# Moving the spatial bias from TensorE to VectorE in a two-layer decoder step, with a new order of gate evictions, row loads, softmax and projection

## The chip, the cores and the metric

The kernel runs on one core of one Trainium2 chip. The metric is the device time of one launch in microseconds (us), the median of several runs; lower is better. The engines: TensorE (PE, matmuls and transposes), VectorE (DVE), ScalarE (ACT), GpSimd (POOL, here mostly gathers and scatters by indirect DMA), SyncE (SP, issues most loads). Each engine runs its own queue of instructions in order, and the kernel ties them together with semaphores by hand.

## The reference, cut

One step of a two-layer decoder for 512 prompt tokens and 8 x 8 sample tokens, 576 rows of 1024. Layer 0 has the chunked gMLP mixer, layer 1 a short convolution; each layer then has 16 experts (two per token) and a per-layer-embedding gate.

```python
# layer 0's mixer; chunks of 128 rows, 4 heads, width 3072
z = gelu(x @ w_in + b_in);  u, v = split(z)
v = layer_norm(v, ln_g, ln_b)
sg = einsum("hts,bcshd->bcthd", tril(w_s), v) + transpose(b_s)[:, :, None]
mix = (u * sg) @ w_out
# every layer
x = layer_norm(alpha * x + mixer(x), ln1_g, ln1_b)
g_logits = x @ w_group + b_group;  e_logits = x @ w_expert + b_expert
# best of 4 groups, two best of its 4 experts; weight = softmax of the two * softmax of the group
moe = sum over the two experts e of weight_e * (silu(x @ w_gate_e) * (x @ w_up_e)) @ w_down_e
x = layer_norm(alpha * x + moe, ln2_g, ln2_b)
x = x + sigmoid(x @ ple_w_gate + ple_b_gate) * (p @ ple_w_proj)
```

## The kernel before, in words

**Numbers.** Every fp32 operand of a matmul is split into a high and a low part of a shorter type (x_hi, x_lo, w_hi, w_lo): ScalarE makes the high part (hi, L848), VectorE the low part (lo, L1166), and PE makes three products per term (L1741 to L1743, L2062 to L2064). Weights come in units of 1 MB (w_raw), which SP loads as their buffers come free, and each unit is split by one hi and one lo of 2048 columns.

**Stages.** V part of the mixer (to 176 us), then six rounds of four tiles of the A width (to 499), then the last output rows with first LayerNorm and router (to 575), 16 experts (to 737), addition of the experts' rows, second LayerNorm and gate (to 820); layer 1 has its convolution and then the same stages from the router on, with the same code, and each is some 501.6 us behind its place in layer 0.

**The mixer's rounds.** For each tile fl of a round PE makes u (u_tile) and the spatial product (spatial, L1854 to L1859) into PSUM banks b and b+1. The head's bias is put there first, by two matmuls of ones_r (all ones, one contraction row that holds the bias) with b_spatial. VectorE's gate_product multiplies u by it in place (L1257, L1258), ScalarE makes the high part (L902), g_low the low part (L1265). PE's out_tiles begins with the first three tiles' products for two output tiles (36 matmuls) before it waits for the fourth tile's low part.

**Router.** h_turns(i) transposes row tile i, logits(i) multiplies by the router's weights; the tiles 0 to 4 follow each other, 4 being the 64 rows left over. Then PE has the projection p @ w_proj in eight tiles (proj), among which stand ranks(1) (L1960, L1963: each token's rank in its expert, from the one-hot that VectorE writes at L1372) and the matmuls L2019 that turn ranks to slots. VectorE makes slot indices from them (L1430), GpSimd gathers the first expert's rows.

**Experts.** moe_step(s): ScalarE splits two weight units, then Silu on gate (L1003), VectorE multiplies by up (L1499), PE transposes the product (L2091), and then has gate_up of the next expert (L2062). Ahead of the first expert VectorE computes the softmax weights (L1457 to L1483), ScalarE two exponentials (L974, L976).

**Second LayerNorm and gate.** y_out copies an expert's result (L987, L989), GpSimd scatters it to y_scratch in DRAM. SP loads the four gate units (gate_load) and the rows of y (rows_load, one per row tile, both experts of each token). VectorE adds the rows (add_rows, L1572) and the last two experts' rows through PE (add_last, L1580; their low parts are L1560 and L1629), ScalarE the squares (L1046) and the standard deviation (L1051). The norm is on ScalarE (L1056) for tiles 0, 2, 3, 4 and on VectorE (L1590) for tile 1. PE turns the rows (n2_turn_rows, L2183), both scale them into xT, and 16 gate tiles follow: q 0 to 7 are the eight output tiles for the first 256 rows, 8 to 15 for the other 320. Tiles q and q+4 share a PSUM bank of the first eight, in its two halves. ScalarE evicts each by a sigmoid (L1081), VectorE finishes it (L1618, L1619).

Of the kernel before, what the change touches and what calls it, by code (L numbers as in the profile page):

```python
# [5 lines left out]
P = 128  # L6
D = 1024
KT = D // P
TP, TS = 512, 64
T = TP + TS  # L10
NT = 5
HALF = T // 2
AW = 3072
NH = 4
# [63 lines left out]
def trunk(nc, x_in, outs):  # L78
# [63 lines left out]
    bsx = new("b_spatial", [P, NH, P + TS], f32r)  # L142
# [21 lines left out]
    bsrc = at("b_spatial_src", [1, NH, P], f32, S0 + 23040)  # L164
    bss = at("b_spatial_all", [1, NH, P + TS], f32, S0 + 25088)
    bsl = at("b_spatial_low", [1, NH, P + TS], f32r, S0 + 28160)
# [5 lines left out]
    gf = at("g_full", [P, 2, T], f32, S0 + 18432)  # L172
    vc = at("v_cols", [P, NT, 512], f32, S0 + 23040)
# [138 lines left out]
    with ctx:  # L312
# [9 lines left out]
        blk_ld, bsl_ld = sem("blocks_loaded"), sem("bias_low_loaded")  # L322
# [12 lines left out]
        bs_ok, bsh_ok, bsl_ok, ones_ok = sem("bias_spread"), sem("bias_high"), sem("bias_low"), sem("ones_ready")  # L335
# [154 lines left out]
        HALVED = (0, 1, 3, 4)  # L490
# [15 lines left out]
        def _(sp):  # L506
# [40 lines left out]
            for l in range(DEPTH):  # L547
# [42 lines left out]
                for j in range(3):  # L590
                    gate_load(j)
# [65 lines left out]
        def _(pool):  # L657
# [20 lines left out]
            pool.dma_start(bsrc[:, :, :], x_in["a_b_s"]).then_inc(ws_ld, 16)  # L678
# [46 lines left out]
            pool.wait_ge(bsl_ok, 1)  # L725
            pool.dma_start(bsx[1:2, :, :], bsl[:, :, :]).then_inc(bsl_ld, 16)
            pool.wait_ge(bsl_ld, 16)
# [27 lines left out]
            for l in range(DEPTH):  # L755
# [47 lines left out]
                for s in range(4, NE):  # L803
                    gather(s)
                    expert_rows(s - 4)
                    if s in (6, 9):
                        n = (s - 6) // 3
                        pool.wait_ge(w_ok, 2 * (l + 1))
# [33 lines left out]
        def _(act):  # L842
# [37 lines left out]
            act.wait_ge(bs_ok, 1)  # L880
            act.activation(bsx[0:1, :, :], bss[:, :, :], ACT.Copy).then_inc(bsh_ok, 1)
# [45 lines left out]
            for l in range(DEPTH):  # L927
# [11 lines left out]
                def proj_out(mo):  # L939
                    act.wait_ge(mt_done, M_P[l] + mo + 1)  # L940
# [22 lines left out]
                rows_hi(4)  # L963
                proj_out(0)
                proj_out(1)
# [5 lines left out]
                xT_hi(0, bank=4)  # L971
                proj_out(KT - 1)
# [3 lines left out]
                act.activation(gm[:, 1, :], gm[:, 1, :], ACT.Exp).then_inc(r_ex_ok, 1)  # L976

# [83 lines left out]
                def scale(i):  # L1061
                    t, b = tok(i), turned_bank(TR_N2[l] + i)
                    act.wait_ge(n2_turn, NT * l + i + 1)
                    for k in range(0 if i == 2 else 4, KT):
# [5 lines left out]
                def tile_hi(i):  # L1070
                    if i != 2:
                        act.wait_ge(n2_scaled, 4 * l + HALVED.index(i) + 1)
# [1239 lines left out]
```

## Time and profile before

| | |
|---|---|
| median of 3 runs | 1335.91 us (1332.87 to 1340.4) |
| profiled execution: its own time, span | 1331.28 us, 1329.7 us |
| mean granted TensorE clock | 0.971 |
| busy: PE, VectorE, ScalarE, GpSimd | 94%, 61%, 44%, 16% |
| moved by DMA | 229.52 MB |

Busy time is the share of the span in which an engine executes something. The clock is a share of 2.4 GHz; a stretch in which it is near 0.5 runs at 1.2 GHz.

### The profile page before, as it was taken

How to read it: one execution, taken by the hardware profiler on the slowest of the kernel's cores; microseconds unless marked ns; L12 is line 12 of the kernel's file. 1: busy time of each engine (PE TensorE's matmuls, PEld its weight loads, DVE VectorE, ACT ScalarE, POOL GpSimd, SP SyncE). 2: the span in 40 equal slices, each digit the busy share in tenths (PEclk: the TensorE clock that was granted, in tenths of full speed). 3: DMA queues.
4: the chain of work that ended last, by engine and by line, in shares of the span. 5: the costliest groups of instructions: out<-in, count | busy, mean ns of one | idle time of the engine just before them, and what ended most of it. 6: DMA issues, size and time to landing. Idle time of an engine off the chain costs nothing.

```text
span 1329.7 us, 19763 instructions
## 1 busy us (share of the span) xinstructions
PE 1254.0 (94%) x7729; PEld 1144.1 (86%) x7729; DVE 815.8 (61%) x1093; ACT 584.6 (44%) x650; POOL 213.6 (16%) x211
## 2 busy tenths in 40 slices
PE   6999999999999999989999599999999989999598
PEld 5888899999999998878878589999998878877488
DVE  4653476254453624779889766455434778888763
ACT  4322241212121223378888663212213368888661
POOL 2300011000000005322331001000004432232000
PEclk8999999999999999899999799999999899999799
DMA  9354344233242312379999453222312279998412
GB/s 315 130 180 140 130 145 143 80 127 114 75 146 75 122 68 66 104 286 349 374 386 337 159 163 100 70 91 80 110 67 66 87 276 348 385 393 323 172 49 71
DMA packets 85664, 229.52 MB, mean 173 GB/s; under 512 B 9878, under 2 KB 42814, under 8 KB 73184
## 3 DMA queue, kind: packets, MB, share of 16 engines
q1 hardware_dynamic: 66880, 179.84, 37.7%
q0 software_dynamic: 18720, 48.80, 10.6%
q8 instruction: 44, 0.72, 0.2%
q14 instruction: 20, 0.16, 0.0%
HBM read 209.90 MB, written 35.46 MB: 185 GB/s over the span
## 4 chain that ended last, share of the span: by engine, by line
PE 70%; DVE 11%; DMA 10%; ACT 6%; issue 2%; SPq 0%; DVEq 0%; ACTq 0%; POOLq 0%
PE ps L1741 13%; PE ps L1743 13%; PE ps L1742 13%; DMA w_raw<-in_moe_w_gate_up 5%; DVE w_lo L1166 3%; PE ps L1793 3%; PE ps L1794 3%; PE ps L1795 3%; DMA w_raw<-in_moe_w_down 2%; ACT w_hi L848 2%; PE ps L2062 2%; PE ps L2063 2%; PE ps L2064 2%; PE ps L1857 2%; DVE x_tok L1572 1%
## 5 line engine op out<-in xcount | busy, mean ns | idle before, releaser
L1166 DVE TENSOR_TENSOR w_lo<-w_raw,w_hi 128x2048 fp32r<-128x2048 f32 (+1 forms) x133 | 290.7, 2191 | 80.6 <-ACT w_hi L848 79.8
L1741 PE MATMUL ps<-x_hi,w_hi 128*128 128x288 f32 (+2 forms) x1024 | 308.6, 301 | 14.7 <-DVE x_lo L1606 8.6
L1743 PE MATMUL ps<-x_hi,w_lo 128*128 128x288 f32 (+2 forms) x1024 | 305.8, 299 | 0.0
L1742 PE MATMUL ps<-x_lo,w_hi 128*128 128x288 f32 (+2 forms) x1024 | 305.7, 299 | 0.0
L848 ACT ACTIVATE w_hi<-w_raw 128x2048 fp32r<-128x2048 f32 (+1 forms) x133 | 242.8, 1834 | 104.5 <-PE ps L1743 73.9
L1741 PEld LDWEIGHTS ps<-x_hi,w_hi 128*128 128x128 f32 x1024 | 196.7, 192 | 17.4 <-issue 15.8
L1742 PEld LDWEIGHTS ps<-x_lo,w_hi 128*128 128x128 f32 x1024 | 196.8, 192 | 0.0
L1743 PEld LDWEIGHTS ps<-x_hi,w_lo 128*128 128x128 f32 x1024 | 196.6, 192 | 0.0
L1741 PE MATMUL ps<-g_hi,w_hi 128*128 128x288 f32 x384 | 114.3, 298 | 3.4 <-DVE g_full L1717 2.7
L1743 PE MATMUL ps<-g_hi,w_lo 128*128 128x288 f32 x384 | 113.2, 295 | 0.0
L1742 PE MATMUL ps<-g_lo,w_hi 128*128 128x288 f32 x384 | 113.1, 295 | 0.0
L2062 PE MATMUL ps<-w_hi,xgT_hi 128*128 128x512 f32 x256 | 104.4, 408 | 8.4 <-DVE xgT_lo L1451 8.1
L2064 PE MATMUL ps<-w_hi,xgT_lo 128*128 128x512 f32 x256 | 101.4, 396 | 0.0
L2063 PE MATMUL ps<-w_lo,xgT_hi 128*128 128x512 f32 x256 | 101.1, 395 | 0.0
L1257 DVE TENSOR_TENSOR g_full<-g_full,ps 128x512 f32<-128x512 f32 x24 | 16.4, 685 | 118.9 <-PE ps L1859 118.9
L1793 PE MATMUL ps<-w_hi,x_hi 128*128 128x512 f32 x192 | 76.1, 396 | 5.7 <-DVE w_lo L1177 5.7
L897 ACT ACTIVATE g_full<-ps,cols 128x576 f32<-128x576 f32 x24 | 17.7, 737 | 135.9 <-PE ps L1743 135.9
L1741 PEld LDWEIGHTS ps<-g_hi,w_hi 128*128 128x128 f32 x384 | 72.0, 188 | 5.6 <-DVE g_full L1717 2.9
L786 POOL DMA_INDIRECT x_gathered<-x_scratch,slot_token x32 | 51.5, 1609 | 152.1 <-PE ps L2033 121.5
L1166 DVE TENSOR_TENSOR w_lo<-w_raw_more,w_hi 128x2048 fp32r<-128x2048 f32 x30 | 68.0, 2289 | 12.2 <-ACT w_hi L848 12.2
L1794 PE MATMUL ps<-w_lo,x_hi 128*128 128x512 f32 x192 | 75.4, 393 | 0.0
L1795 PE MATMUL ps<-w_hi,x_lo 128*128 128x512 f32 x192 | 75.4, 393 | 0.0
(311 smaller groups left out, 2313.4 us busy)
## 6 DMA issues: line engine op xcount, KB each, us to landing
w_raw<-in_moe_w_gate_up SPq DMA_DIRECT2D x34, 1024.0 KB, 9.9
w_raw<-in_moe_w_down SPq DMA_DIRECT2D x32, 1024.0 KB, 13.9
w_raw_more<-in_moe_w_gate_up SPq DMA_DIRECT2D x30, 1024.0 KB, 14.6
w_raw<-in_a_w_in SPq DMA_DIRECT2D x23, 1024.0 KB, 5.3
w_raw<-in_a_w_out SPq DMA_DIRECT2D x12, 1024.0 KB, 5.1
w_raw<-in_b_w_in SPq DMA_DIRECT2D x12, 1024.0 KB, 5.2
w_raw<-in_ple_w_gate SPq DMA_DIRECT2D x8, 1024.0 KB, 10.2
v_scratch<-v_stage POOLq DMA_DIRECT2D x6, 1024.0 KB, 4.8
```

The costliest lines, as they stand in the source:

```text
L786: pool.indirect_dma_start(out=xg[:, s % 2, :], out_offset=None, in_=x_dram[l][:, :], in_offset=bass.IndirectOffsetOnAxis(ap=idx[:, s:s + 1 ...
L848: act.activation(unit_of(whi, d), raw_unit(d), ACT.Copy).then_inc(hi_done, 1)
L1166: dve.tensor_tensor(unit_of(wlo, d), raw_unit(d), unit_of(whi, d).bitcast(f32), ALU.subtract).then_inc(split_done, 1)
L1741: pe.matmul(out, sh, mh, start=first, stop=False)
L1742: pe.matmul(out, sh, ml, start=False, stop=False)
L1743: ins = pe.matmul(out, sl, mh, start=False, stop=final)
L1793: pe.matmul(v_bank(i), xh_, wh, start=first, stop=False)
L1794: pe.matmul(v_bank(i), xh_, wl, start=False, stop=False)
L1795: ins = pe.matmul(v_bank(i), xl_, wh, start=False, stop=final)
L2062: pe.matmul(ps[:, 0, :], xs[0], ws[0], start=(a == 0 and k == 0), stop=False)
L2063: pe.matmul(ps[:, 0, :], xs[0], ws[1], start=False, stop=False)
L2064: ins = pe.matmul(ps[:, 0, :], xs[1], ws[0], start=False, stop=(a == 1 and k == 3))
```

## The change

1. The bias b_s is loaded once by a broadcasting DMA to all 128 partitions. PE's two bias matmuls per tile go, and so does the preparation of the bias (its high and low part on VectorE and ScalarE, a DMA, two waits). gate_product adds the bias to the spatial product from PSUM to a new tile gate_sum and then multiplies u by it.
2. Gate tiles are evicted in the order 0, 4, 1, 5, 2, 6, 3, 7, 8 to 15 (EVICTED), and gate(8) to gate(11) wait for 2, 4, 6, 8 evictions instead of 5, 6, 7, 8. The turns of tile 4 come behind gate(6) instead of gate(5).
3. The norm of tiles 2 to 4 goes to VectorE, and so does half of the scaling of tile 2.
4. SP issues gate_load(2) behind rows_load(1), and VectorE adds the first rows ahead of the last experts' low parts.
5. Softmax: the last experts' places and the group's softmax stand ahead of the first rows' low part on VectorE, the exponentials ahead of their high part on ScalarE; ScalarE loads the Silu table by a one-column activation before it waits for the first gate_up.
6. Projection tile 1 is made in two halves, around h_turns(4).

```diff
 # SP
-                for j in range(3):
+                for j in range(2):
                     gate_load(j)
...
                 rows_load(1)
+                gate_load(2)
 # POOL
+            pool.dma_start(bs[:, :, :], x_in["a_b_s"].to_broadcast([P, NH, P])).then_inc(bs_ld, 16)
 # ACT
+                    if s == 0 and not step:
+                        act.activation(warm[:, :], eps[:, :], ACT.Silu)
                     q = it * step + (NE * l + s)
                     act.wait_ge(eu_used, it * (3 * step) + (EU * l + gu_unit(s) + 2))
...
+                proj_out(1)
                 proj_out(0)
-                proj_out(1)
...
-                xT_hi(0, bank=4)
-                proj_out(KT - 1)
                 act.wait_ge(r_ex, 2 * l + 1)
                 act.activation(ex[:, :, :], ex[:, :, :], ACT.Exp).then_inc(r_ex_ok, 1)
                 act.wait_ge(r_ex, 2 * l + 2)
                 act.activation(gm[:, 1, :], gm[:, 1, :], ACT.Exp).then_inc(r_ex_ok, 1)
+                xT_hi(0, bank=4)
+                proj_out(KT - 1)
...
                 squares(2)
                 std_of(2)
-                norm(2)
                 squares(3)
                 std_of(3)
                 scale(2)
-                norm(3)
                 tile_hi(2)
+                hi(U_G[l] + 3)
                 squares(4)
                 std_of(4)
-                norm(4)
-                hi(U_G[l] + 3)
 # DVE, gate_product
-                dve.wait_ge(u_done, q + 1)
+                b = 4 + 2 * (fl % 2)
                 dve.wait_ge(sg_done, q + 1)
-                b = 4 + 2 * (fl % 2)
-                dve.tensor_tensor(gf[:, fl % 2, 0:TP], gf[:, fl % 2, 0:TP], ps[:, b, :], ALU.mult)
-                dve.tensor_tensor(gf[:, fl % 2, TP:T], gf[:, fl % 2, TP:T], ps[:, b + 1, 0:TS], ALU.mult).then_inc(gm_done, 1)
+                dve.tensor_tensor(gsum[:, 0:TP].rearrange("p (c t) -> p c t", t=P), ps[:, b, :].rearrange("p (c t) -> p c t", t=P), bias, ALU.add)
+                ch.link(dve.tensor_tensor(gsum[:, TP:T].rearrange("p (b t) -> p b t", t=SB),
+                                          ps[:, b + 1, 0:TS].rearrange("p (b t) -> p b t", t=SB), bias_s, ALU.add))
+                dve.wait_ge(u_done, q + 1)
+                dve.tensor_tensor(gf[:, fl % 2, :], gf[:, fl % 2, :], gsum[:, :], ALU.mult).then_inc(gm_done, 1)
 # PE, spatial
-                pe.matmul(ps[:, b, :].rearrange("p (c t) -> p c t", t=P), ones_r[:, :], row, start=True, stop=False)
-                pe.matmul(out_s, ones_r[:, :], row_s, start=True, stop=False)
 # PE, router
                 logits(3)
+                pe.wait_ge(nz_ok, 2 * NT * l + NT - 1)
+                proj_half(l, 1, 0)
                 h_turns(4)
+                proj_half(l, 1, 1).then_inc(mt_done, 1)
                 logits(4)
                 pe.wait_ge(nz_ok, 2 * NT * l + NT)
                 proj(l, 0)
-                proj(l, 1)
                 ranks(1)
 # PE, gate
                     if q >= KT:
-                        pe.wait_ge(sg_ok, GQ * l + q - 3)
+                        pe.wait_ge(sg_ok, GQ * l + (2 * (q - KT) + 2 if q < KT + 4 else q - 3))
...
-                    if q in (1, 4, 5):
-                        n2_turn_rows((1, 4, 5).index(q) + 2)
+                    if q in (1, 4, 6):
+                        n2_turn_rows((1, 4, 6).index(q) + 2)
```

The first place is VectorE's queue in the mixer's first round, around the first two tiles' gate products (g_full is u and then the product, g_lo its low part). Before:

```order
L1257 TENSOR_TENSOR g_full<-g_full,ps 128x512
L1258 TENSOR_TENSOR g_full<-g_full,ps 128x64
L1166 TENSOR_TENSOR w_lo<-w_raw,w_hi 128x2048
L1265 TENSOR_TENSOR g_lo<-g_full,g_hi 128x576
L1257 TENSOR_TENSOR g_full<-g_full,ps 128x512
```

and after, where the lines of the file have other numbers:

```order
L1244 TENSOR_TENSOR gate_sum<-ps,b_spatial 128x512
L1245 TENSOR_TENSOR gate_sum<-ps,b_spatial 128x64
L1248 TENSOR_TENSOR g_full<-g_full,gate_sum 128x576
L1159 TENSOR_TENSOR w_lo<-w_raw,w_hi 128x2048
L1255 TENSOR_TENSOR g_lo<-g_full,g_hi 128x576
```

Two multiplies from PSUM have become two additions from PSUM and one multiply between tiles in SBUF; the weight split and the low part follow as they did.

The second place is SP's queue between the experts' last weights and the rows of y (w_raw<-in_ple_w_gate is a gate unit, the loads from y_scratch are the row tiles 0, 1, 2). Before, with the overflow branch, which isn't taken, left out:

```order
L587 DMA w_raw<-in_ple_w_gate 128x8x256 [waits w_split_done] x3
...
L615 DMA w_raw_more<-y_scratch 128x2x1024 [waits zeros_stored,w_split_done,y_stored1,y_stored0]
L615 DMA x_gathered<-y_scratch 128x2x1024 [waits xg_turned]
L615 DMA w_raw<-y_scratch 128x2x1024 [waits w_split_done,y_stored1,y_stored0]
L615 DMA w_raw<-y_scratch 128x2x1024
```

and after:

```order
L585 DMA w_raw<-in_ple_w_gate 128x8x256 [waits w_split_done] x2
...
L613 DMA w_raw_more<-y_scratch 128x2x1024 [waits zeros_stored,w_split_done,y_stored1,y_stored0]
L613 DMA x_gathered<-y_scratch 128x2x1024 [waits xg_turned]
L585 DMA w_raw<-in_ple_w_gate 128x8x256 [waits w_split_done]
L613 DMA w_raw<-y_scratch 128x2x1024 [waits w_split_done,y_stored1,y_stored0]
```

The third gate unit has moved behind two row loads and behind their wait for stores of y.

The third place is VectorE's queue behind the last expert (last_y_lo is the low part of the last two experts' rows, x_tok the row tile). Before:

```order
L1560 SCALAR_TENSOR_TENSOR last_y_lo_166<-expert_y,slot_weight,last_y_hi_164 128x1024
L1629 SCALAR_TENSOR_TENSOR last_y_lo_167<-ps,slot_weight,last_y_hi_165 128x512 x2
L1572 SCALAR_TENSOR_TENSOR x_tok<-w_raw_more,top_weights,x_tok 128x1024 x2
L1580 SCALAR_TENSOR_TENSOR x_tok,row_sums<-ps,x_tok 128x1024
L1565 TENSOR_SCALAR mean_var<-row_sums 128x1
L1572 SCALAR_TENSOR_TENSOR x_tok<-x_gathered,top_weights,x_tok 128x1024
L1592 RECIPROCAL rstd<-rstd 128x1
L1593 TENSOR_TENSOR neg_mean_rstd<-mean_var,rstd 128x1
L1572 SCALAR_TENSOR_TENSOR x_tok<-x_gathered,top_weights,x_tok 128x1024
```

and after:

```order
L1559 SCALAR_TENSOR_TENSOR x_tok<-w_raw_more,top_weights,x_tok 128x1024
L1616 SCALAR_TENSOR_TENSOR last_y_lo_164<-expert_y,slot_weight,last_y_hi_162 128x1024
L1559 SCALAR_TENSOR_TENSOR x_tok<-w_raw_more,top_weights,x_tok 128x1024
L1622 SCALAR_TENSOR_TENSOR last_y_lo_165<-ps,slot_weight,last_y_hi_163 128x512 x2
L1559 SCALAR_TENSOR_TENSOR x_tok<-x_gathered,top_weights,x_tok 128x1024
L1567 SCALAR_TENSOR_TENSOR x_tok,row_sums<-ps,x_tok 128x1024
L1552 TENSOR_SCALAR mean_var<-row_sums 128x1
L1559 SCALAR_TENSOR_TENSOR x_tok<-x_gathered,top_weights,x_tok 128x1024
L1579 RECIPROCAL rstd<-rstd 128x1
L1580 TENSOR_TENSOR neg_mean_rstd<-mean_var,rstd 128x1
```

Both additions of tile 0 and the first of tile 1 have moved up, among the low parts; the second of tile 1 stands ahead of tile 0's reciprocal.

## Rows read from the trace of the kernel before

**Rows 1.** The page, part 4: shares of the chain that ended last
```profile
PE 70%; DVE 11%; DMA 10%; ACT 6%; issue 2%; SPq 0%; DVEq 0%; ACTq 0%; POOLq 0%
```
**Rows 2.** Windows: us, busy of PE, PEld, DVE, ACT, POOL, clock, DMA share, GB/s
```profile
186.00:499.00 313.00, 312.37 (x2304) 304.45 (x2302) 149.43 (x186) 69.04 (x67) 19.45 (x34) 1.00 0.33 109
...
620.00:735.00 115.00, 110.18 (x527) 91.44 (x526) 99.27 (x87) 93.66 (x93) 32.18 (x23) 1.00 0.94 359
```
**Rows 3.** PE's waits, whole run: us in total, times, longest
```profile
PE ps L2183 <- ACT x_tok L1056: 11.8, 2, 5.9
```
**Rows 4.** Timeline of PE, two of the mixer's tiles: start, duration, line, operation
```profile
246.01 0.50 PE L1854 MATMUL ps<-b_spatial,ones_r 128*128 x1
...
246.41 1.10 PE L1857 MATMUL ps<-w_spatial,v_cols 128*128 x8
...
262.54 0.39 PE L1854 MATMUL ps<-b_spatial,ones_r 128*128 x1
...
262.82 1.10 PE L1857 MATMUL ps<-w_spatial,v_cols 128*128 x8
```
**Rows 5.** Timeline of VectorE, the same tile; in brackets the idle time before
```profile
264.45 0.69 DVE L1257 TENSOR_TENSOR g_full<-g_full,ps 128x512 f32<-128x512 f32 x1 [4.30 <-PE ps L1859]
...
266.02 0.76 DVE L1265 TENSOR_TENSOR g_lo<-g_full,g_hi 128x576 fp32r<-128x576 f32 x1 [0.75 <-ACT g_hi L902]
```
**Rows 6.** Timeline of PE, router
```profile
548.05 0.71 PE L1942 MATMUL ps<-ident,x_tok 64*128 64x64 f32 x8 [1.37 <-ACT x_tok L925]
550.17 0.32 PE L1952 MATMUL ps<-w_router_scaled,x1T_hi 128*128 128x120 f32 x1 [1.41 <-DVE x1T_lo L1339]
...
558.38 0.21 PE L1960 MATMUL ps<-expert_onehot,below_r 128*128 128x96 f32 x1
```
**Rows 7.** Windows: router, first experts, gates
```profile
550.00:557.00 7.00, 6.83 (x32) 6.83 (x33) 6.76 (x14) 0.59 (x1) 4.83 (x4) 0.55 0.35 112
...
584.00:588.00 4.00, 3.31 (x9) 2.62 (x9) 4.00 (x5) 2.43 (x3) 0.99 (x2) 0.60 1.02 425
...
789.00:793.00 4.00, 4.00 (x19) 4.00 (x19) 2.34 (x7) 0.95 (x2) 0.00 (x0) 0.58 0.93 292
```
**Rows 8.** Timeline of VectorE, router
```profile
557.11 0.21 DVE L1372 SCALAR_TENSOR_TENSOR expert_onehot<-places,group_onehot 128x48 fp32r<-128x48 f32 x1
```
**Rows 9.** Timeline of ScalarE, first expert
```profile
579.91 1.28 ACT L1003 ACT_TABLE_LOAD   x1
581.21 0.38 ACT L1003 ACTIVATE expert_act<-ps 128x256 f32<-128x256 f32 x1
```
**Rows 10.** Timeline of VectorE, first expert
```profile
583.07 0.41 DVE L1499 TENSOR_TENSOR expert_act<-expert_act,ps 128x256 f32<-128x256 f32 x1
```
**Rows 11.** Timeline of PE, first expert
```profile
584.73 0.72 PE L2062 MATMUL ps<-w_hi,xgT_hi 128*128 128x512 f32 x1 [0.69 <-DVE xgT_lo L1451]
```
**Rows 12.** DMA issues, 724 to 746 and 741 to 746 us: median us to landing
```profile
x_gathered<-y_scratch SPq DMA_DIRECT2D x1, 1024.0 KB, 8.8
...
y_scratch<-expert_y,slot_row POOLq DMA_INDIRECT x1, 7.3
...
y_scratch<-expert_y,slot_row_late POOLq DMA_INDIRECT x1, 3.2
```
**Rows 13.** Timeline of GpSimd, end of the experts
```profile
725.50 1.31 POOL L792 DMA_INDIRECT y_scratch<-expert_y,slot_row  x1 [8.33 <-ACT expert_y L989]
```
**Rows 14.** Timeline of ScalarE, head of the gate stage
```profile
738.33 1.92 ACT L848 ACTIVATE w_hi<-w_raw 128x2048 fp32r<-128x2048 f32 x1
...
743.31 1.15 ACT L1046 ACTIVATE w_raw_more<-x_tok,mean_var 128x1024 f32<-128x1024 f32 x1 [0.64 <-DVE mean_var L1565]
...
748.03 1.15 ACT L1046 ACTIVATE x_gathered<-x_tok,mean_var 128x1024 f32<-128x1024 f32 x1 [1.41 <-DVE mean_var L1565]
```
**Rows 15.** Timeline of VectorE, head of the gate stage
```profile
739.23 2.60 DVE L1572 SCALAR_TENSOR_TENSOR x_tok<-w_raw_more,top_weights,x_tok 128x1024 f32<-128x1024 f32 x2
```
**Rows 16.** Timeline of PE, the ninth gate tile
```profile
788.18 0.38 PE L1741 MATMUL ps<-x_hi,w_hi 128*128 128x320 f32 x1 [3.05 <-ACT ple_gate L1081]
```

More of the change, by code:

```diff
@@ L141, in trunk @@
     wss = new("w_spatial_s", [TS, NH, TS])
-    bsx = new("b_spatial", [P, NH, P + TS], f32r)
+    bs = new("b_spatial", [P, NH, P])
     vstat = new("v_stats", [P, NT, VP, 6])
@@ L172, in trunk @@
     gf = at("g_full", [P, 2, T], f32, S0 + 18432)
+    gsum = at("gate_sum", [P, T], f32, S0 + 37376)
     vc = at("v_cols", [P, NT, 512], f32, S0 + 23040)
@@ L489, in trunk @@
         LAST_BANK = (6, 2)
-        HALVED = (0, 1, 3, 4)
+        EVICTED = (0, 4, 1, 5, 2, 6, 3, 7) + tuple(range(KT, GQ))
         V_DONE = NT * VP
@@ L1063, in scale @@
                     act.wait_ge(n2_turn, NT * l + i + 1)
-                    for k in range(0 if i == 2 else 4, KT):
+                    for k in range(4, KT):
                         c = KT * l + k
@@ L1445, in _ @@
                 dve.tensor_scalar(ovf_e[:, :], ovf_f[0:1, :], float(NE - 1), None, ALU.min).then_inc(ovf_ok, 1)
-                def xT_lo(s, it=0, step=0, bank=2):
-                    q = it * (2 * step) + 2 * (NE * l + s)
-                    for b in range(2):
-                        dve.wait_ge(eth_ok, q + (b + 1))
-                        dve.tensor_tensor(eTl[:, 512 * b:512 * b + 512], ps[:, bank + b, :], eTh[:, 512 * b:512 * b + 512].bitcast(f32),
-                                          ALU.subtract).then_inc(etl_ok, 1)
-                xT_lo(0, bank=4)
+                late_v = row_v[:, NE - 2:NE]
+                ch.link(dve.scalar_tensor_tensor(out=last_at[:, 0, :], in0=shift[:, NE - 2:NE], scalar=float(T), in1=late_v, op0=ALU.add, op1=ALU.subtract))
+                dve.tensor_scalar(last_at[:, 1, :], last_at[:, 0, :], -float(P), None, ALU.add)
+                ch.link(dve.tensor_scalar(last_at[:, 2, :], last_at[:, 0, :], PA - 0.5, 2.0 * T, ALU.is_lt, ALU.mult))
+                ch.link(dve.tensor_tensor(last_at[:, 3, :], last_at[:, 2, :], late_v, ALU.add))
+                dve.tensor_scalar(row_zero[:, :], last_at[:, 3, :], -1.0, 4.0 * T, ALU.mult, ALU.add)
+                dve.scalar_tensor_tensor(out=row_late[:, :], in0=last_at[:, 2, :], scalar=2.0 * T, in1=late_v, op0=ALU.add, op1=ALU.subtract)
                 grp = lg[:, :, 0, :]
@@ L1466, in _, with xT_lo @@
                     dve.tensor_copy(ranks[:, a:b, :], ranks_of(a, b))
+                def xT_lo(s, it=0, step=0, bank=2):
+                    q = it * (2 * step) + 2 * (NE * l + s)
+                    for b in range(2):
+                        dve.wait_ge(eth_ok, q + (b + 1))
+                        dve.tensor_tensor(eTl[:, 512 * b:512 * b + 512], ps[:, bank + b, :], eTh[:, 512 * b:512 * b + 512].bitcast(f32),
+                                          ALU.subtract).then_inc(etl_ok, 1)
+                xT_lo(0, bank=4)
                 dve.wait_ge(r_ex_ok, 2 * (l + 1))
@@ L1650, in _ @@
                 rstd2(3)
+                scale2(2)
                 add_rows(4, 0)
@@ L2035, in turn_slots, with proj_half @@
                         ins.then_inc(xtp, 1)
+            def proj_half(l, mo, h):
+                if h == 0:
+                    pe.wait_ge(split_done, U_P[l] + mo // 2 + 1)
+                return products(ps[:, 2 * (mo % 2) + h, 0:HALF], [(w8(whi, mo // 2, k, P * (mo % 2)), w8(wlo, mo // 2, k, P * (mo % 2)),
+                                                                 gview(pThi, k, h), gview(pTlo, k, h)) for k in range(2)])
             def proj(l, mo):
```

104 lines of the change are left out of this document (41 added, 63 removed).

## Prediction

> **What bounds the kernel now.** I read the chain that ended last first: TensorE (PE) holds 70% of it, VectorE, DMA and ScalarE 11, 10 and 6% [rows 1]. So an edit pays where it takes matmuls from PE, where PE waits, or where PE runs at its lower clock; work taken from another engine alone pays nothing. Second, the windows by stage [rows 2]: from 186 to 499 us (the rounds of layer 0's mixer) PE is busy 312.37 of 313 us, so only fewer matmuls help there. In the experts (620 to 735) it is busy 110.18 of 115, and the DMA share is 0.94 at 359 GB/s, so two resources are almost full. Third, PE's waits over the whole run: the largest, twice 5.9 us since there are two layers, is for tile 0's normalised rows ahead of the per-layer gate [rows 3]. Last, the timelines around each place that the change touches; all times below are layer 0's, and layer 1 repeats the stages from the router on, so those terms count twice.
>
> The profiled execution took 1331.28 us (span 1329.7), which is 4.6 us under the median of the three timed runs, 1335.91, and 1.6 under the lowest. The sum is made against 1331.28. How much of the 4.6 the next runs have I can't know, and I add half of it at the end. No change that can be measured is within 0.5%, 6.7 us.
>
> **1. Spatial bias.** On PE the bias matmul of a tile starts at 262.54 and the first spatial one at 262.82, so the two bias matmuls cost 0.28 us of issue; after another spatial tile it is 0.40 (246.01 to 246.41), one tile of four [rows 4]. 18 x 0.28 + 6 x 0.40 = 7.4 us over 24 tiles, all on a PE that never idles. I take -7.3 (range -6, if a few tenths of every round come back as waits, to -7.6). VectorE pays for it. Now it multiplies from PSUM, 0.69 us for the 512 columns and 0.82 with the other 64 (264.45 to 265.27, where its idle time begins), waits 0.75 for the high part and subtracts in 0.76, which ends at 266.78, 2.3 us in all [rows 5]. After, there are two adds from PSUM, for which I take the same 0.82 (their bias operand is read repeated, which no row shows, so up to 1.3), and a multiply of 128x576 between SBUF tiles, for which the subtraction of that shape (0.76) is nearest. The chain becomes 3.1 us, up to 3.6. Who waits? The last tile of a round is needed only after 36 matmuls of the output products, and at 312.37 us for 2304 matmuls [rows 2] these take 4.9 us: 1.3 to 1.8 us are left. The other three tiles have a whole u tile (48 matmuls) before theirs is wanted. So the adds cost nothing while that slack is there; if it were gone, each 0.1 us of overrun would cost 6 x 0.1 us.
>
> **2. Router and projection.** After logits(3) PE idles 1.37 us for the norm of tile 4 and, after its turns, 1.41 us for its low part, with a clock of 0.55 from 550 to 557 [rows 6, 7]. The edit puts half of projection tile 1 (12 matmuls, 1.6 us at 0.136 each) into each idle stretch. About 1.4 of the 2.8 us of idle are filled (the first half can start late, behind a turned PSUM bank), logits(4) runs at full clock, and PE is done with projections 0 and 1 near 553.6 instead of 558.38. But ranks(1), L1960, needs the expert one-hot, which VectorE writes at 557.11 to 557.32 [rows 8] behind the slot one-hots of the earlier tiles and the logits of tile 4, none of which moves. The stall goes there: a gap of about 3.7 us before ranks(1), in which the clock can fall, as it did behind the two gaps now. Without a fall ranks(1) starts 1.0 us sooner (-0.95 on the gather of the first rows). With a fall, ranks(1), projection 2 and the slot matmuls, some 3.3 us of PE work to the slot indices, run at the rate of 0.55, which lasts longer. I take +1.0, range -0.95 to +1.9.
>
> **3. Softmax and the Silu table.** Now VectorE does fourteen small operations between the first gathered rows and the first weight split, and ScalarE loads the Silu table at 579.91, for 1.28 us, right when gate_up(0) is done [rows 9]. VectorE's product of the first activation starts at 583.07 without idle time before it [rows 10], behind two splits that follow ScalarE's; PE waits for it and then 0.69 us for the next rows' low part, until 584.73 [rows 11], and runs its first 4 us at a clock of 0.60 [rows 7]. After, the two exponentials come before the first rows' high part, and the table is loaded ahead of that wait. ScalarE's high part of the first weights starts right after proj_out(7), where a table load and two exponentials (1.5 us) stand now. VectorE's small operations end 0.6 us after that high part now, and after the change they no longer do: its splits follow 1.5 + 0.6 = 2.1 us sooner, and gate_up(1) starts 2.1 us sooner, near 582.65. PE's idle time there nearly vanishes; if the clock then holds, 4 us at 0.60 give back 1.6 more, together 3.8. The later experts are bound by weight loads as much as by PE [rows 2], and those are released by splits that come only 1.5 to 2.1 us sooner, so not all arrives. I take -3.0, range -2.1 to -3.8. The Trainium skill ("ScalarE: Activation LUTs", What ACT_TABLE_LOAD costs) puts a table switch at 1.28 us of load plus about 1.4 of drain. The trace agrees with the first number and shows no drain: the Silu follows its load by 0.02 us [rows 9]. By the page's sum this step would be worth some 1.4 us more per layer, by the row it is not.
>
> **4. Head of the gate stage.** SP now issues the third gate unit before the rows of y, and the scatter of expert 13 (7.3 us), which the row loads wait for, flies beside it; the second row load takes 8.8 [rows 12]. After, the unit is issued third. Its landing W: scatter 13 starts at 725.50 [rows 13] and lands between 728.7 (3.2 us, the last scatter, which flies nearly alone) and 732.8 (as now); 0.4 us later come the two row loads, 8.8 us, and then 1 MB more at the 359 GB/s of [rows 2], 2.9 us. So W is 740.8 to 744.9, middle 742.8, against the 738.33 at which ScalarE splits this unit now. And this split still stands ahead of the last expert's eviction, the Sigmoid table's load and the squares of tile 0 on ScalarE's queue [rows 14]: ScalarE waits up to 4.5 us with all of these behind it, and PE waits for them through L2183. From the split's start to the squares it is 4.98 us less 0.64 idle, 4.34. From squares(0) to squares(1) it is 4.72 us, less 1.31 since one of the two y additions there (2.60 us a pair [rows 15]) is moved forward: 3.41. squares(1) thus start at W + 7.75, that is at 750.55 instead of 748.03: +2.5 us. The break-even is W = 740.3. The gain on the other side, if W stays below that, is at most ScalarE's idle 0.64 ahead of squares(0) and the 1.3 of the moved addition, -1.9. Range -1.9 to +4.6. Behind that, scale2(2) and the norms of tiles 2 to 4 go from ScalarE to VectorE beside PE's gate matmuls of the first half; they matter for the next part alone.
>
> **5. End of the gates.** gate(8) needs the bank of gate 0 or 4 evicted, and waits 3.05 us for the fifth eviction, which ScalarE does behind tile 4's squares, norm, scale and high part; then the clock is 0.58 from 789 to 793 [rows 16, 7]. After, evictions go 0, 4, 1, 5, and gate(8) needs the first two, which lie ahead of tile 4's high part. It can follow the turns of tile 4 as soon as x_lo(4) is there, 2.5 us sooner, and without idle time the 4 slow microseconds give 1.6 back: -4.1, range -3.0 to -4.5.
>
> **Sum.** -7.3 + 2 x (1.0 - 3.0 + 2.5 - 4.1) = -7.3 - 7.2 = -14.5, so 1316.8, and with half of the 4.6, **1319 us**.
>
> **Rivals.**
> - Forecast as above, own range 1312 to 1326: 0.41.
> - The head of the gates pays: scatter 13 lands early and W stays near 740. For it: the scatter's 3.2 us when alone. Against: 3 MB have to come in behind it. Part 4 gives -1.5 or so instead of +2.5: 1319 - 8 = 1311. 0.16.
> - The experts swallow their part: weight loads, 0.94 of the DMA time, release each expert when they did before, and 2 x 3.0 are lost: 1325. For it: PE still idles 4.8 of 115 us there. Against: until 620 us PE hardly waits. 0.18.
> - The unit lands at 744.9 or later: 2 x 2.1 more, 1323. 0.08.
> - The adds' chain ends last in the mixer: if the repeated bias operand is read slowly and the chain exceeds 4.9 us by 1 us in each of six rounds, 6 of the 7.3 are lost: 1325. Against: it needs the adds at four times their rows. 0.06.
> - Little changes: a new gap of 3.7 us before ranks(1) keeps the clock down to the gather, and parts 3 and 4 come out at their bad ends; 1330 to 1338. 0.07.
> - Slower: one mechanism, the third gate unit. ScalarE waits for it with the last eviction behind, whose store the last rows of y wait for, and with it PE. The price is 1 us per microsecond of W past 740.3, twice. Without part 4 the sum stands at 1314.1 (half of the 4.6 in it), and 1342.6 is 28.5 above that: it decides from W = 740.3 + 28.5/2 = 754.5, ten microseconds past the top of my bounds; with W at 756 the kernel takes 1345. 0.04.
>
> So faster 0.89, within 0.5% 0.07, slower 0.04. The range 1307 to 1331 leaves out about half a chance in ten at each end: the cases of little change and slower above it, and the good head with good ends elsewhere below it.
>
> **What would show it.** (1) rounds of the mixer 1.2 us shorter each, no wait of PE on g_lo. (2) no 1.4 us waits at L1942 and L1952, but one of 3 to 4 us at L1960, half clock after it. (3) the first gate_up(1) 2.1 us sooner relative to the first gathered rows, the clock at 1 from 584. (4) ScalarE waiting 3 to 5 us for the DMA of the third gate unit before its split, squares(0) later. (5) no wait of gate(8) on an eviction. I am wrong if the third unit lands early or very late, or if the expert stage's length grows by what its entry gains.

## The result and the profile after

| | before | after | ratio, 95% interval |
|---|---|---|---|
| median | 1334.39 us (4 runs) | 1313.59 us (1311.79 to 1317.97, 4 runs) | 0.985 (0.982 to 0.9879) |
| the change run again later | 1333.73 us (11 runs) | 1313.40 us (5 runs) | 0.9849 (0.983 to 0.9869) |
| span of the profiled execution | 1329.7 us | 1311.8 us | |

The page of the changed kernel (busy time by engine, then the shares of the chain that ended last) answers to [rows 1]:

```profile
PE 1242.1 (95%) x7681; PEld 1132.3 (86%) x7681; DVE 837.0 (64%) x1118; ACT 576.2 (44%) x637; POOL 208.9 (16%) x210
...
PE 74%; DMA 11%; DVE 8%; ACT 5%; issue 2%; SPq 0%; DVEq 0%; POOLq 0%; ACTq 0%
```

PE has 48 matmuls fewer and 12 us less of busy time, VectorE 21 us more, and VectorE's share of the chain fell all the same, from 11 to 8%: added work that nobody waits for is not in the chain.

The time came from the places that the prediction named. I laid the two traces' landmarks side by side (first row of a stage on PE), and took differences from one to the next:

| stretch, from ... to ... | predicted, per layer | layer 0 | layer 1 |
|---|---|---|---|
| start to the first spatial matmul | 0 | +0.7 | |
| six mixer rounds | -7.3 | -7.8 | |
| to tile 4's turns in the router | 0 | -1.6 | +3.1 |
| to the first gathered rows | +1.0 | +0.5 | 0.0 |
| to the last expert's down product | -3.0 | -3.7 | -4.3 |
| to gate(0) | +2.5 | +2.3 | +2.3 |
| to the end of the layer's gates | -4.1 | -4.8 | -4.7 |

Before rounding they add up to -17.9, which is the difference of the spans.

PE's waits over the whole run, of the changed kernel (us in total, times, longest), against [rows 3]:

```profile
PE ps L2178 <- ACT x_tok L1052: 15.1, 2, 7.6
PE ps L1733 <- DVE x_lo L1593: 8.6, 2, 4.3
...
PE ps L1947 <- DVE expert_onehot L1363: 2.2, 2, 1.1
...
PE ps L1733 <- DVE w_lo L1159: 1.6, 2, 0.8
```

The wait for tile 0's normalised rows grew from 5.9 to 7.6 us per layer. The gate's wait for an eviction (3.05 us, [rows 16]) is gone; what is left in the gates is 0.8 us for a weight split, at an earlier gate (768.69). The wait for the expert one-hot is new. The wait for x_lo at gate(0), 4.3 us per layer, is as before.

**The mixer.** VectorE's timeline for the fourth tile of the second round:

```profile
262.70 0.69 DVE L1244 TENSOR_TENSOR gate_sum<-ps,b_spatial 128x512 f32<-128x512 f32 x1 [3.18 <-PE ps L1846]
263.31 0.21 DVE L1245 TENSOR_TENSOR gate_sum<-ps,b_spatial 128x64 f32<-128x64 f32 x1
263.56 0.76 DVE L1248 TENSOR_TENSOR g_full<-g_full,gate_sum 128x576 f32<-128x576 f32 x1
265.07 0.76 DVE L1255 TENSOR_TENSOR g_lo<-g_full,g_hi 128x576 fp32r<-128x576 f32 x1 [0.75 <-ACT g_hi L896]
```

The chain is 3.13 us, from 262.70 to 265.83, as counted; the repeated bias operand costs nothing (0.69 us, as the multiply from PSUM did in [rows 5]). VectorE still idles 3.18 us before it.

**Head of the gate stage.** ScalarE's timeline, and PE's first two turns of rows:

```profile
725.26 1.27 ACT L978 ACTIVATE last_y_hi<-ps,slot_weight 128x512 fp32r<-128x512 f32 x2 [0.40 <-PE ps L2076]
730.80 1.91 ACT L844 ACTIVATE w_hi<-w_raw 128x2048 fp32r<-128x2048 f32 x1 [4.27 <-DMA w_raw<-in_ple_w_gate]
732.61 1.01 ACT L981 ACTIVATE expert_y<-ps 128x1024 f32<-128x1024 f32 x1
733.64 1.28 ACT L1085 ACT_TABLE_LOAD   x1
734.93 0.20 ACT L1085 ACTIVATE warm<-eps 128x1 f32<-128x1 f32 x1
735.04 1.13 ACT L1042 ACTIVATE w_raw_more<-x_tok,mean_var 128x1024 f32<-128x1024 f32 x1
...
738.42 1.15 ACT L1042 ACTIVATE x_gathered<-x_tok,mean_var 128x1024 f32<-128x1024 f32 x1
```
```profile
738.47 1.94 PE L2178 MATMUL ps<-ident,x_tok 128*128 128x128 f32 x8 [7.62 <-ACT x_tok L1052]
741.09 1.97 PE L2178 MATMUL ps<-ident,x_tok 128*128 128x128 f32 x8 [0.68 <-DVE x_tok L1577]
```

ScalarE stands still for 4.27 us until the third gate unit has landed, at 730.80. The last expert's down product is 11.93 us earlier in this trace than before (722.19 against 734.12), so in the time of [rows 14] that is 742.7, and the prediction had put W at 742.8; squares(1) start 7.62 us behind it, for 7.75. The last eviction, the table load and the squares all stand behind it.

### The profile page after: what moved, and what is told of

The parts are those of the page before. It is cut to its first block, busy times and chain, and to the rows that moved or that the text cites. A ratio compares the mean times of both kernels' runs of the same rounds, so it can differ in the third digit from the quotient of the medians.

```text
span 1311.8 us, 19697 instructions
## 1 busy us (share of the span) xinstructions
PE 1242.1 (95%) x7681; PEld 1132.3 (86%) x7681; DVE 837.0 (64%) x1118; ACT 576.2 (44%) x637; POOL 208.9 (16%) x210
## 4 chain that ended last, share of the span: by engine, by line
PE 74%; DMA 11%; DVE 8%; ACT 5%; issue 2%; SPq 0%; DVEq 0%; POOLq 0%; ACTq 0%
PE ps L1733 14%; PE ps L1735 14%; PE ps L1734 14%; DMA w_raw<-in_moe_w_gate_up 7%; PE ps L1785 3%; PE ps L1786 3%; PE ps L1787 3%; DVE w_lo L1159 2%; ACT w_hi L844 2%; PE ps L2057 2%; PE ps L2059 2%; PE ps L2058 2%; PE ps L1844 2%; DMA w_raw<-in_ple_w_gate 2%; PE ps L2022 1%
## 5 line engine op out<-in xcount | busy, mean ns | idle before, releaser
L1244 DVE TENSOR_TENSOR gate_sum<-ps,b_spatial 128x512 f32<-128x512 f32 x24 | 16.5, 689 | 97.0 <-PE ps L1846 97.0
L1735 PEld LDWEIGHTS ps<-g_hi,w_lo 128*128 128x128 f32 x384 | 72.7, 189 | 0.0
L1734 PEld LDWEIGHTS ps<-g_lo,w_hi 128*128 128x128 f32 x384 | 72.7, 189 | 0.0
## 6 DMA issues: line engine op xcount, KB each, us to landing
w_raw<-in_ple_w_gate SPq DMA_DIRECT2D x8, 1024.0 KB, 11.9
```

The costliest lines, as they stand in the source:

```text
L1734: pe.matmul(out, sh, ml, start=False, stop=False)
L1735: ins = pe.matmul(out, sl, mh, start=False, stop=final)
```

## The experiments

Each kernel ran beside runs of the kernel before on the same chip. "Head" is PE's time from the last expert's down product to gate(0): before 22.83 us in both layers, after 25.15 and 25.09.

**bias_only: part 1 alone.** The kernel before with the edits to `spatial`, `gate_product` and the bias's preparation, and none of the others:

```diff
-                pe.matmul(ps[:, b, :].rearrange("p (c t) -> p c t", t=P), ones_r[:, :], row, start=True, stop=False)
-                pe.matmul(out_s, ones_r[:, :], row_s, start=True, stop=False)
...
+                dve.tensor_tensor(gsum[:, 0:TP].rearrange("p (c t) -> p c t", t=P), ps[:, b, :].rearrange("p (c t) -> p c t", t=P), bias, ALU.add)
```

> The kernel before with the bias part alone (no bias matmuls, two adds on VectorE). My theory: PE drops 24 pairs of bias matmuls out of rounds in which it never idles, 0.28 us each and 0.40 for one tile of four, and VectorE's longer chain is hidden: rounds of 58.7 us become 57.4, the time falls by 7.3 us against the kernel before, and nothing behind the rounds changes length. Rival 1: the adds' chain ends last in some tiles, PE waits on g_lo, and less than 4 us come. Rival 2: the bias part is worth more than its matmuls, since the changed kernel's stretch from the last mixer round to the router's last turns was 1.6 us shorter too; then 9 us.

Measured: 1323.95 us against 1333.09, ratio 0.9919 (0.989 to 0.9949), 6.8 to 14.7 us; the profiled spans differ by 7.4 (1322.3 against 1329.7). PE shows no wait for g_lo, so rival 1 is out. The six rounds are 7.8 us shorter, as in the changed kernel. Whether the part is worth 7.4 or the 9 of rival 2 the interval doesn't decide; but the 1.6 us that rival 2 points at are a fall of the clock that the trace of the kernel before has there (last section), and not a gain of the edit.

**split_late: ScalarE splits the third gate unit after tile 1's high part.** SP's order stays as changed.

```diff
                     if s == NE - 1:
                         for h in range(2):
...
-                        hi(U_G[l] + 2)
                         act.wait_ge(yl_ok, 3 * (l + 1))
...
                 tile_hi(1)
+                hi(U_G[l] + 2)
                 squares(2)
```

> The changed kernel, but ScalarE splits the third gate unit behind the high part of tile 1 instead of ahead of the last expert's eviction. In the changed kernel ScalarE waits 4.27 us for this unit's DMA (split at 730.80) with the eviction, the table load and the squares of tile 0 behind it; VectorE had tile 0's mean at 731.9, and squares(0) start at 735.04. My theory: that wait sets the head of the gate stage; squares(0) start near 732.0 and squares(1) near 735.4 instead of 738.42, 3.0 us sooner in each layer, 6 us in all, 1307.6. Rival: VectorE's order of additions sets it, and the time stays within 2 us of the changed kernel's. Second rival: the late split delays the gates of unit 2 and takes back 2 us or more per layer.

Measured: 1309.47 us, ratio 0.9821 (0.9785 to 0.9857), and measured again, beside the changed kernel on one chip, 1309.98 (6 runs) against 1313.40 (5 runs). The head is 22.41 and 22.08 us, 2.7 and 3.0 less than the changed kernel's. ScalarE's timeline:

```profile
731.60 1.03 ACT L980 ACTIVATE expert_y<-ps 128x1024 f32<-128x1024 f32 x1 [3.12 <-DVE last_y_lo L1622]
...
734.25 1.15 ACT L1041 ACTIVATE w_raw_more<-x_tok,mean_var 128x1024 f32<-128x1024 f32 x1
...
745.07 1.89 ACT L844 ACTIVATE w_hi<-w_raw 128x2048 fp32r<-128x2048 f32 x1
749.16 1.15 ACT L1041 ACTIVATE w_raw<-x_tok,mean_var 128x1024 f32<-128x1024 f32 x1 [2.20 <-DVE mean_var L1552]
```

The split now lies in time in which ScalarE waits for tile 2's mean anyway (2.20 us are left of it). The wait for the unit was what lengthened the head. The medians give only 3.4 to 4.1 of the 5.7 us that the two heads gain. Its profile loses 2.6 us to a long low clock at the router of layer 0 (below); whether the timed runs lost time in the same way isn't known.

**unit_early: the third unit back ahead of the rows of y.**

```diff
-                for j in range(2):
+                for j in range(3):
                     gate_load(j)
...
                 rows_load(1)
-                gate_load(2)
```

> The changed kernel with the third gate unit issued where it was before, ahead of the rows of y. ScalarE then finds it landed, but the scatter of expert 13 and the row loads behind it land later, as in the kernel before (rows 0 five microseconds after 732.8). My theory: VectorE begins its additions some 2 us later and becomes what sets squares(1), so that of the 2.3 us that the head lost only about 1.1 come back per layer, 2 us in all: 1311.5. Rival: the whole loss and the moved additions' gain come, 3 us per layer: 1307.5. Second rival: the early rows were the gain, and it is slower than the changed kernel by 1 us or more per layer.

Measured: 1317.4 us, ratio 0.9873 (0.9838 to 0.9909): slower than the changed kernel by 3.8 us in the medians. Only the first half of my theory held: additions later, but at a place that I had not counted. VectorE and PE in layer 0:

```profile
727.07 1.28 DVE L1558 SCALAR_TENSOR_TENSOR x_tok<-w_raw_more,top_weights,x_tok 128x1024 f32<-128x1024 f32 x1 [4.12 <-DMA w_raw_more<-y_scratch]
728.39 1.28 DVE L1615 SCALAR_TENSOR_TENSOR last_y_lo<-expert_y,slot_weight,last_y_hi 128x1024 fp32r<-128x1024 f32 x1
```
```profile
729.82 0.77 PE L2113 MATMUL ps<-last_y_hi,last_onehot 128*128 128x512 f32 x1 [3.79 <-DVE last_y_lo L1615]
```

The changed order puts the addition of the first rows ahead of the last experts' low part on VectorE. With the rows late, that low part queues behind a DMA, and PE waits for it: 3.79 us in layer 0, 3.11 in layer 1 (1.57 and 1.65 in the changed kernel, no such wait before). The head is 26.68 us in layer 0, where the clock fell during this wait (0.60 from 728 to 730, then 0.50 to 734), and 23.63 in layer 1, where it held until 1240.

The two heads together take 50.3 us, as in the changed kernel (50.2). So they don't explain the 3.8 us of the medians, whose cause stays open: the two traces differ by 4.4 us, 3.1 of them from tile 4's turns to the last expert in layer 1, where the clock was low for 17 us at the router. What is shown is that VectorE's new order makes PE wait when SP's order is the old one (the reverse was not tried); the place to mend the wait for the unit is ScalarE's queue.

**old_evict: the order of evictions undone, the norms left on VectorE.**

```diff
-        EVICTED = (0, 4, 1, 5, 2, 6, 3, 7) + tuple(range(KT, GQ))
+        EVICTED = tuple(range(GQ))
...
-                        pe.wait_ge(sg_ok, GQ * l + (2 * (q - KT) + 2 if q < KT + 4 else q - 3))
+                        pe.wait_ge(sg_ok, GQ * l + q - 3)
...
-                    if q in (1, 4, 6):
-                        n2_turn_rows((1, 4, 6).index(q) + 2)
+                    if q in (1, 4, 5):
+                        n2_turn_rows((1, 4, 5).index(q) + 2)
```

> The changed kernel with gate tiles evicted in the order 0 to 15, gate(8) to gate(11) waiting for 5 to 8 evictions and tile 4's turns behind gate(5) again; the norms stay on VectorE. The gate stage was 4.7 us shorter in each layer. My theory: the order does it, since gate(8) waits for the fifth eviction, 2.5 us, and the clock falls behind that gap, 1.6 us: about 4 us per layer come back, 1321.8, with a wait of 3 us at the ninth gate and a clock near 0.6 behind it. Rival: ScalarE, freed of three norms, evicts soon enough in the old order: within 2 us of the changed kernel.

Measured: 1322.76 us, ratio 0.9927 (0.9906 to 0.9947), 9.2 above the changed kernel. The gates of layer 0 take 3.5 us longer and those of layer 1 3.4, close to the 4 expected. But the gap is not where I had put it:

```profile
771.36 0.68 PE L2178 MATMUL ps<-ident,x_tok 64*128 64x64 f32 x8 [1.80 <-DVE x_tok L1577]
...
780.49 0.38 PE L1733 MATMUL ps<-x_hi,w_hi 128*128 128x320 f32 x1 [1.02 <-ACT ple_gate L1077]
```
```profile
774.00:778.00 4.00, 4.00 (x29) 4.00 (x28) 2.33 (x6) 1.11 (x2) 0.00 (x0) 0.76 1.10 356
...
780.00:784.00 4.00, 3.51 (x24) 3.54 (x25) 3.81 (x10) 1.77 (x4) 0.00 (x0) 1.00 1.10 348
```

(The second fence shows windows: PE busy comes first behind the length, the granted clock third from the end.) Tile 4's turns, one gate earlier here, wait 1.80 us for its norm, and the ninth gate waits only 1.02 for its eviction: ScalarE without three norms is sooner. The two positions, of the turns and of the evictions, were undone together, so their shares are not told apart; the wait at the turns already brings the clock down to 0.76. The gates account for 6.9 of the 9.2 us. In the profile the router and experts of layer 0 take 3.0 us longer too (185.8 against 182.8), with a low clock of 10 us behind the ranks; that lies ahead of everything that this edit changes.

**no_softmax: part 5 undone.**

```diff
-                act.wait_ge(r_ex, 2 * l + 1)
-                act.activation(ex[:, :, :], ex[:, :, :], ACT.Exp).then_inc(r_ex_ok, 1)
...
                 xT_hi(0, bank=4)
                 proj_out(KT - 1)
+                act.wait_ge(r_ex, 2 * l + 1)
+                act.activation(ex[:, :, :], ex[:, :, :], ACT.Exp).then_inc(r_ex_ok, 1)
...
-                        act.activation(warm[:, :], eps[:, :], ACT.Silu)
```

and on VectorE xT_lo(0) ahead of the group's softmax, the last places behind it, as before.

> The changed kernel without the softmax part: exponentials, last places and softmax stand where they were, and no early load of the Silu table. From the first gathered rows to the last expert the changed kernel was 3.7 us shorter in layer 0 and 4.25 in layer 1. My theory: this part does all of it, through the first gate_up (2.1 us sooner) and the clock behind the gap: 1313.6 + 8 = 1321.6. Rival: the weight loads set the experts' end, and only 2 us per layer or less are lost, 1317. I expect idle times of 1.7 and 0.7 us back at the first expert's transposes and gate_up.

Measured: 1322.15 us, ratio 0.9916 (0.9889 to 0.9944), 8.6 above the changed kernel. The waits are back at 575.55 (1.71 us, transposes) and 576.75 (0.69, gate_up). From the first gathered rows to the last expert it takes 5.1 us longer in layer 0, but only 1.9 in layer 1. Windows of 4 us around the start of gate_up(1): this kernel in layer 0 and in layer 1, then the changed one in layer 0:

```profile
576.00:580.00 4.00, 3.31 (x10) 2.53 (x10) 4.00 (x5) 2.44 (x3) 1.00 (x2) 0.65 1.01 423
...
1080.00:1084.00 4.00, 3.31 (x16) 2.59 (x16) 4.00 (x5) 2.62 (x3) 1.16 (x2) 1.00 0.99 414
```
```profile
574.00:578.00 4.00, 3.77 (x17) 3.04 (x17) 3.08 (x4) 3.78 (x4) 1.72 (x2) 1.00 0.90 344
```

In layer 0, 10 matmuls begin in the one and 17 in the other: the gap costs itself and the clock behind it. In layer 1 the gap is the same (1.75 and 0.69 us) and the clock held. Either way gate_up(1) starts 13.6 us behind the first gathered rows, against 11.4: 2.2 us in each layer. The rest of the way to the last expert is 2.9 us longer in layer 0 and 0.3 shorter in layer 1. So of the 2.2 the weight loads took back 0.3 at most, and the larger half of layer 0's loss is the clock, which does not always fall.

**no_halves: projection tile 1 whole again.**

```diff
                 logits(3)
-                pe.wait_ge(nz_ok, 2 * NT * l + NT - 1)
-                proj_half(l, 1, 0)
                 h_turns(4)
-                proj_half(l, 1, 1).then_inc(mt_done, 1)
                 logits(4)
                 pe.wait_ge(nz_ok, 2 * NT * l + NT)
                 proj(l, 0)
+                proj(l, 1)
```

> The changed kernel without the split projection: tile 1 whole and behind tile 0, as before. From tile 4's turns to the first gathered rows the changed kernel was 0.46 us longer in layer 0 and equal in layer 1. My theory: the halves only move the stall to the ranks, since the one-hot comes from VectorE at the same time, and keep the clock low longer; without them the time is the same or up to 1 us less, 1312.6 to 1313.6, with waits of 1.4 and 1.4 us back ahead of tile 4's turns and logits and none at the ranks. Rival: the gaps' filling pays and its loss costs 2 us per layer, 1317.5.

Measured: 1313.07 us, ratio 0.9851 (0.9808 to 0.9894), the changed kernel's time. The halves are worth nothing that can be measured. The waits behave as expected (1.37 and 1.41 us back, none at the ranks).

**adds_2 and adds_4: how much room VectorE has.** The 512-column addition gets two or four extra repetitions in every tile, which write the same values. Each kernel ran once. The edit of adds_4:

```diff
+                for _ in range(4):
+                    ch.link(dve.tensor_tensor(gsum[:, 0:TP].rearrange("p (c t) -> p c t", t=P), ps[:, b, :].rearrange("p (c t) -> p c t", t=P), bias, ALU.add))
```

> The changed kernel with the 512-column addition done three times in every tile (the two extra ones write the same values), each waiting for the one before: some 1.5 us more in the chain from the spatial product to g_lo. My theory gives 1.3 to 1.8 us of slack ahead of the fourth tile's last products, so PE waits at most 0.2 us a round; no change. Rival: the slack is smaller, PE waits for g_lo in every round, 1 us each, 6 in all.

> The same with four extra additions, some 3.0 to 3.2 us more in the chain. My theory: 1.3 to 1.8 us over the slack, in six rounds 8 to 11 us more than the changed kernel, seen as a wait of PE for g_lo once a round at the output products. Rival: the chain has far more room than I counted, since the following tiles give the time back: no change.

Measured: adds_2 1312.3 us, no wait for g_lo. adds_4 1355.22 us, 42 above the changed kernel, where I expected 8 to 11. PE's waits between 180 and 540 us, and one of them:

```profile
PE ps L1735 <- DVE g_lo L1257: 20.5, 5, 4.3
PE ps L1911 <- DVE g_lo L1257: 5.4, 2, 4.3
```
```profile
257.69 2.86 DVE L1245 TENSOR_TENSOR gate_sum<-ps,b_spatial 128x512 f32<-128x512 f32 x4
...
263.63 2.86 DVE L1245 TENSOR_TENSOR gate_sum<-ps,b_spatial 128x512 f32<-128x512 f32 x4
...
270.93 2.86 DVE L1245 TENSOR_TENSOR gate_sum<-ps,b_spatial 128x512 f32<-128x512 f32 x4
```

The additions of the second, third and fourth tile start with no idle time before them: VectorE's queue is full, and each tile hands its delay to the next. I had counted the last tile's chain alone. The room is a sum over the round: in the changed kernel VectorE idles 1.77 us before the third tile and 3.18 before the fourth, and behind that the last low part has some 1.6 us; 6.5 us in all against 4 x 2.87 = 11.5 added. That makes 5 us per round, up to 4.3 were measured, and the clock is lower with these waits (mean 0.96 from 186 to 499 us, against 1.00). The waits are 26 us. By the landmarks, the six rounds take 30.0 us longer (335.3 against 305.3) and the stretch from there to tile 4's turns 10.0, together 40 of the 42. So about 14 us come on top of the waits in these two stretches, with the clock below 1 in both (0.96 and 0.91); what share is the clock's was not separated.

**both, and the same two again.** Late split and no halves together, beside the late split and the changed kernel, on one chip.

> The changed kernel with the third gate unit split late and projection tile 1 whole again. The late split gave 3.0 us per layer at the head of the gate stage (22.1 to 22.4 us from the last expert's down product to gate 0, against 25.1). With the halves the low clock behind the first gap of the router lasted 10 or 16 us in most profiles, without them 7 us in both layers. My theory: the two add up, and the long low stretch (2.7 us in one layer of two) goes: 1306 to 1308. Rival: the halves are worth nothing either way, and it is level with the late split alone.

> The late split alone once more, on the same chip as the version with both: 1308 to 1310, if the low stretch in the router is again 16 us long in some executions and 10 in others; 1307.5 if it is always short here.

> The changed kernel once more on the same chip: 1313.6, six us above the late split, if ScalarE's wait for the third gate unit is what the late split removes.

Measured: both 1307.16 us (ratio 0.9815, 0.9794 to 0.9837), split_late_again 1309.98 (0.9818, 0.9795 to 0.984), after_again 1313.4. The head of `both` is 22.2 and 22.1 us. It has the lowest median, but its ratio is level with the late split's, so only the late split is shown to gain.

**Why the router's clock matters.** Windows of the low stretch: the kernel without halves, the late split (first profile), and the late split (second profile), which waits at the ranks; behind them that wait as PE's timeline shows it in the changed kernel's second profile.

```profile
540.00:547.00 7.00, 6.82 (x30) 6.82 (x31) 6.76 (x14) 0.21 (x1) 4.87 (x4) 0.52 0.36 112
```
```profile
541.00:557.00 16.00, 15.02 (x67) 14.67 (x68) 12.50 (x28) 3.18 (x4) 5.56 (x5) 0.51 0.34 115
```
```profile
541.00:551.00 10.00, 5.92 (x47) 5.15 (x45) 9.48 (x15) 4.75 (x5) 6.04 (x4) 1.00 0.42 147
551.00:557.00 6.00, 5.52 (x32) 5.52 (x33) 4.08 (x17) 0.65 (x1) 0.00 (x0) 0.72 0.12 16
```
```profile
547.07 0.45 PE L1947 MATMUL ps<-expert_onehot,below_r 128*128 128x96 f32 x1 [3.60 <-DVE expert_onehot L1363]
```

Without halves the clock was low for some 7 to 11 us behind the first gap, in every layer looked at. With halves there are three courses for one program: low for 10 us, low for 16 us, or full up to the ranks and low for 3 to 10 us behind the gap there. The long low stretches are the costly ones: from tile 4's turns to the last expert's down product it takes 185.5 us with the second course (late split, layer 0) and 185.8 with 10 us behind the ranks (old order of evictions, layer 0), against 182.0 with the first (late split, layer 1).

## Why the prediction was right

The forecast was 1319 us, with a range of 1307 to 1331, and 1313.6 was measured. The steps hold one by one, as below; the number is 5 us high, and half of the 4.6 us that were added at the end for the medians' distance from the profiled run did not come: the changed kernel's median and its profiled run agree (1313.59 and 1313.36).

1. **Bias, -7.3.** Right by its own steps: 7.8 us less in the rounds, a chain of 3.13 us for the 3.1 counted, no wait. The slack was worked out wrongly as that of one chain; it is that of a queue, and adds_4 shows the difference. It did not matter at the size of this change.
2. **Router, +1.0.** It came out at +0.5 and 0.0. The stall did go to the ranks: 3.56 to 3.61 us in the ten stretches of all these profiles in which the clock held until there (predicted 3.7), 1.0 to 1.3 where slowed matmuls fill it, as in both layers of the changed kernel's first profile. One step was wrong: I had written 12 matmuls and 1.6 us for a half; the order shows 6, so 0.8 us, and two halves fill 1.8 of the 2.8 us. And logits(4), said to run at full clock, did not in that profile: the clock fell behind the waits of 0.5 and 0.4 us that are left, ahead of the ranks and not behind them. That the term came out near its size although the clock took three courses is in part luck.
3. **Softmax, -3.0.** -3.7 and -4.3, the top of the range and a little beyond. I had let the weight loads take back 0.8. gate_up(1) starts 2.2 us sooner in both layers (2.1 forecast), and the rest of the experts is 1.5 and 2.1 us shorter, where 1.6 had been put on the clock: nothing was taken back. no_softmax shows the first part in both layers and the second in layer 0 alone, since its clock did not fall in layer 1. The Trainium skill puts a drain of about 1.4 us beside each table load ("ScalarE: Activation LUTs", What ACT_TABLE_LOAD costs), by which, as an estimate, the step would have gained 1.4 more. The loads here are again followed by their activation at once (Silu 570.04 + 1.28, next 571.33; at the head 733.64 + 1.28, next 734.93), so no drain is among the causes.
4. **Head, +2.5.** +2.3 in both layers, with the landing within 0.1 us of the middle of the bounds. split_late shows that this wait alone made it.
5. **Gates, -4.1.** -4.8 and -4.7. The two mechanisms (a wait and the clock behind it) were right; old_evict puts the part of the order and of the turns' place at 3.5 and 3.4; the rest may be the norms' move, which was not tried alone.

The sum was -14.5, the traces differ by -17.9 (the medians by -20.8, where single runs of one kernel lie up to 6 or 9 us apart). Over both layers term 3 is off by -1.9, term 2 by -1.5, term 5 by -1.2, term 1 by -0.5 and term 4 by -0.4, together -5.6; the start and the clock falls of the last section give +2.2 the other way. That these two partly cancel is luck.

## What to carry to other kernels

When a load is moved behind others, look for the instruction that first waits for it and at what stands behind that instruction on its queue: here a weight split that nobody needed yet held an eviction, a table load and a LayerNorm, and moving one line took 3 us off each head and 3.4 us off the median. When work is added to an engine with idle time, count the idle time of its whole round and not that of the one chain at its end: here two extra additions per tile fitted in and four did not. Before filling a PE gap, look whether the work behind it is held by another engine; here it was, and the gap moved.

## What the runs showed that was not expected

The clock also falls where PE never idles. Windows of the kernel before, 24 us ahead of tile 4's turns in layer 0, where PE makes output rows and the first router matmuls (columns as above):

```profile
522.00:524.00 2.00, 2.00 (x18) 1.79 (x17) 0.31 (x2) 1.20 (x1) 0.00 (x0) 0.85 0.00 0
524.00:526.00 2.00, 2.00 (x10) 2.00 (x11) 0.29 (x1) 0.35 (x2) 0.01 (x1) 0.50 0.00 0
526.00:528.00 2.00, 2.00 (x12) 1.86 (x11) 1.01 (x1) 0.95 (x1) 2.00 (x1) 0.80 0.00 0
```

and of the changed kernel at the same place of layer 1:

```profile
1012.00:1014.00 2.00, 2.00 (x16) 1.81 (x15) 0.03 (x2) 1.48 (x2) 0.00 (x0) 0.79 0.03 8
1014.00:1016.00 2.00, 2.00 (x12) 2.00 (x11) 0.27 (x1) 0.43 (x1) 0.39 (x1) 0.50 0.00 0
```

Both times PE was busy 2.00 of 2 us with transposes and small router matmuls; the other layer of the same trace has no such fall. The first accounts for the -1.6 in the table. The second and a fall behind a gap that both kernels have account for the +3.1: PE waits 2.68 us for g_full early in layer 1's output products, in both traces, and behind it the clock held before and fell after:

```profile
952.00:955.00 3.00, 3.00 (x24) 3.00 (x24) 1.88 (x5) 0.44 (x1) 0.00 (x0) 1.00 0.89 322
```
```profile
938.00:941.00 3.00, 3.00 (x15) 3.00 (x14) 1.88 (x5) 0.07 (x1) 0.00 (x0) 0.51 0.79 320
```

So an equal gap does not always bring an equal clock. Each of these falls costs about 1.6 us: from this wait to tile 4's turns it takes 97.2 us in the kernel before, with neither fall, 98.7 or 98.8 in the four traces with one, and 100.3 or 100.4 in the eight with both. The trace of the kernel before is the only one of the thirteen with neither, so the +3.1 is that trace's good luck and no cost of the change.

The second thing is the start: PE's first product of weights began between 11.9 and 14.8 us in these traces and the first spatial one between 184.3 and 187.0, 2.7 us in all. Two traces of one program differ there by 1.6 us (the changed kernel) and 1.8 us (the late split), so this is no effect of an edit. A difference of 2 us between two single traces of this kernel proves nothing; between the same stretch in both layers and several traces it does.
